# A fused two-block network kernel: the FFN written as two program blocks instead of one, and another order of the group norm around the last scan chunk

## The reference

```
y  = (scan + d_skip * xs) * silu(z)
yg = y * rsqrt(mean(y*y over the group) + eps) * norm_g
x  = x + gate * (yg @ out_w)
```

## Time and profile before

| | |
|---|---|
| median of 3 runs | 1453.96 us (1452.37 to 1456.07) |
| the profiled execution | 1453.96 us, span 1452.2 us |
| PE busy | 94% of the span |
| DVE, ACT, POOL busy | 57%, 41%, 28% |
| mean granted TensorE clock | 0.967 of full speed |
| DMA | 181 MB, mean 125 GB/s |

### The profile page before, as it was taken

How to read it: one execution, slowest core, us unless ns; L and a number is a source line. 1 busy time by engine, 2 the same in 40 slices (tenths; PEclk the granted TensorE clock), 3 DMA queues, 4 the chain that set the end, 5 groups by cost and what they waited for, 6 DMA issues and landing times. The chain is left out here.

```text
span 1452.2 us, 19530 instructions
## 1 busy us (share of the span) xinstructions
PE 1364.5 (94%) x7904; PEld 1080.3 (74%) x7904; DVE 820.9 (57%) x965; ACT 589.0 (41%) x848; POOL 409.3 (28%) x191
## 2 busy tenths in 40 slices
PE   5999789969999999999999998998999999999996
PEld 3777566748888888887778886766777799777775
DVE  3788763476556555333755665776842831565544
ACT  4323445442222222212454346776632422455541
POOL 0000000018987888999200000000000050232220
PEclk9999889979999999999799999999999999999998
DMA  9433035213544545554132333334132342111121
GB/s 390 148 145 117 30 109 182 66 51 120 215 186 166 186 167 222 204 182 174 58 120 87 114 109 105 117 102 151 38 110 88 127 163 88 58 47 42 59 88 58
DMA packets 41350, 181.12 MB, mean 125 GB/s; under 512 B 3392, under 2 KB 20160, under 8 KB 21312
## 3 DMA queue, kind: packets, MB, share of 16 engines
q1 hardware_dynamic: 40128, 171.73, 32.9%
q10 hardware_dynamic: 1152, 8.39, 1.7%
HBM read 173.75 MB, written 6.36 MB: 124 GB/s over the span
## 5 line engine op out<-in xcount | busy, mean ns | idle before, releaser
L193 DVE TENSOR_TENSOR wlo<-raw,whi 128x2048 fp32r<-128x2048 f32 x95 | 253.7, 2670 | 182.2 <-ACT whi L189 179.6
L200 POOL TENSOR_TENSOR ada_raw<-ada_raw,cs 128x2048 f32<-128x2048 f32 x36 | 150.1, 4171 | 504.2 <-DVE h2lo L451 457.5
L271 PE MATMUL ps<-hhi,whi 128*128 128x512 f32 x640 | 252.1, 394 | 2.3 <-PEq L562 0.8
L271 PE MATMUL ps<-hhi,wlo 128*128 128x512 f32 x640 | 249.4, 390 | 0.0
L271 PE MATMUL ps<-hlo,whi 128*128 128x512 f32 x640 | 249.1, 389 | 0.0
L189 ACT ACTIVATE whi<-raw 128x2048 fp32r<-128x2048 f32 x95 | 181.5, 1911 | 143.6 <-PE ps L1303 91.3
L209 POOL TENSOR_TENSOR ada_raw<-ada_raw 128x1024 f32<-128x1024 f32 x72 | 164.4, 2283 | 5.7
L271 PEld LDWEIGHTS ps<-hhi,whi 128*128 128x128 f32 x640 | 120.2, 188 | 28.7 <-issue 2.4
L271 PEld LDWEIGHTS ps<-hhi,wlo 128*128 128x128 f32 x640 | 120.1, 188 | 25.7
L271 PEld LDWEIGHTS ps<-hlo,whi 128*128 128x128 f32 x640 | 120.2, 188 | 24.3
L2030 POOL TENSOR_TENSOR x<-x,rest 128x256 f32<-128x256 f32 (+3 forms) x32 | 49.0, 1531 | 163.8 <-DVE rest L2325 163.8
(11 more groups left out here) (373 smaller groups left out, 2810.1 us busy)
## 6 DMA issues: line engine op xcount, KB each, us to landing
raw<-panels SPq DMA_DIRECT2D x87, 1024.0 KB, 4.9
ada_raw<-ada SPq DMA_DIRECT2D x48, 1024.0 KB, 6.7
first<-ada SPq DMA_DIRECT2D x8, 1024.0 KB, 20.7
bc<-ac_rows SPq DMA_DIRECT2D x32, 256.0 KB, 3.8
raw<-panels ACTq DMA_DIRECT2D x8, 1024.0 KB, 5.1
x_kept<-x SPq DMA_DIRECT2D x2, 2048.0 KB, 9.6
x<-x_kept SPq DMA_DIRECT2D x2, 2048.0 KB, 8.0
x<-x_in SPq DMA_DIRECT2D x1, 2048.0 KB, 9.1
```

Of the source, the lines that this page charges most:

```text
L193: e.tensor_tensor(wlo[:, c % 2, :, :], raw[:, c % 2, :, :], whi[:, c % 2, :, :].bitcast(F32), ALU.subtract).then_inc(lo_split, 1)
L200: e.tensor_tensor(ada_raw[:, c % 2, :, :], ada_raw[:, c % 2, :, :], cs[:, which, :].unsqueeze(2).to_broadcast([P, KT, 256]), ALU.mult).the ...
L271: mm = e.matmul(ps[:, 2 * (qc % 2) + b, :], w[:, c % 2, 2 * k + b, :], src[part][:, k, :], **flags)
```

## The change

**Edit 1, the FFN.** The one block becomes two: one for the input projection, one for the output projection with its norms. Each engine's stream is cut at the same place, between the last input step and the first output panel. The special order of banks in PE's first output panel goes, and so do its three waits and POOL's wait for the pairs ahead of ada block 50. No arithmetic is added or taken away.

**Edit 2, the scan's last chunk and the group norm.** The arithmetic stays; helpers move within the streams of PE, ACT and DVE. The quarters of `z` in the last chunk move from the steps 1, 3, 5, 6 to 1, 2, 4, 6.

```
@@ the FFN
+                c0 = FIRST["ffn_out"]
+                last = c0 + COUNT["ffn_out"] - 1
...
+                with nc.Block() as block:
...
-                            if a == 50:
-                                pool.wait_ge(pair_free[0], 17)
-                                pool.wait_ge(pair_free[1], 17)
...
-                        pe.wait_ge(lo_split, co + 1)
-                        for b in (5, 6, 7, 0, 1, 2, 3, 4):
-                            if b in (0, 2):
-                                pe.wait_ge(pair_free[b // 2], 17)
-                            if b == 4:
-                                pe.wait_ge(mod_read, read_counts[(20, 41)])
-                            for k2 in range(2):
-                                mm = product(co, 0, k2, b, k2)
-                        mm.then_inc(panels_used, 1)
+                        panel(c0, 0, 0)
@@ the scan
-            IN_BATCHES = [(1, 2, 4, 5, 7), (1, 3, 5, 7), (1, 2, 4), (1, 3, 5, 6)]
+            IN_BATCHES = [(1, 2, 4, 5, 7), (1, 3, 5, 7), (1, 2, 4), (1, 2, 4, 6)]
@@ PE, behind the contraction of a step of the last chunk
-                                        if 2 * g + b == 5:
+                                        if 2 * g + b == 4:
                                             squares(0)
                                         if 2 * g + b == 6:
                                             group_spread(0)
-                                        if 2 * g + b == 7:
                                             squares(1)
@@ PE, in m_panel(k), ahead of tile j
-                                if (k, j) == (0, 2):
+                                if (k, j) == (0, 1):
                                     group_spread(1)
...
-                                if (k, j) == (1, 3):
+                                if (k, j) == (1, 2):
                                     squares(3)
-                                if (k, j) == (2, 1):
+                                if (k, j) == (2, 0):
                                     group_spread(3)
@@ ACT, behind decays(n) of the last chunk
-                                if c == TB - 1 and b == 5:
+                                if c == TB - 1 and b == 4:
                                     group_squares(0)
+                                if c == TB - 1 and b == 6:
+                                    group_squares(1)
@@ ACT, behind the scan
-                        group_squares(1)
                         hi_part(act, 0)
                         group_std(1)
                         for p in late:
                             split_hi(act, c0 + p + 2, 0)
+                        for p in range(turned, MT // 2):
+                            silu_z(p)
                         group_squares(2)
                         hi_part(act, 1)
-                        group_std(2)
-                        for p in range(turned, MT // 2):
-                            silu_z(p)
                         for n in range(NN - 5, NN):
                             for p in taken_at(n):
                                 load_panel(act, c0 + p + 4, 0)
-                        hi_part(act, 2)
+                        group_std(2)
                         group_squares(3)
                         split_hi(act, cm + 2, 0)
+                        hi_part(act, 2)
                         group_std(3)
@@ DVE, in the last chunk
-                                    if g < MG - 1 and not (c == TB - 1 and b == 1):
+                                    if g < MG - 1:
                                         masked(n + 2)
-                                    if g < MG - 1 and c < TB - 1:
                                         for p in taken_at(n - 1) if n % NB else ():
                                             split_lo(dve, c0 + p + 2, 0)
...
-                                    if g < MG - 1:
-                                        masked(c * NB + 2 * g + 3)
                                     if g == MG - 2:
                                         group_rs(dve, 0)
+                                    dve.wait_ge(M["yskip"], 4 * gi + 4)
+                                    if g < MG - 1:
+                                        dve.wait_ge(G["z"], 2 * g + 2)
                                     if g == MG - 1:
-                                        for n in range(NN - 3, NN):
-                                            for p in taken_at(n):
-                                                split_lo(dve, c0 + p + 2, 0)
                                         norm_lo(dve, 1)
-                                        group_rs(dve, 2)
-                                    dve.wait_ge(M["yskip"], 4 * gi + 4)
-                                    dve.wait_ge(G["z"], 2 * g + 2)
+                                        dve.wait_ge(G["z"], 2 * g + 2)
                                     gate_part(dve, g)
-                                    if g == 1:
-                                        for n in range(c * NB, NN - 3):
-                                            for p in taken_at(n):
-                                                split_lo(dve, c0 + p + 2, 0)
...
+                        for n in range(NN - 3, NN):
+                            for p in taken_at(n):
+                                split_lo(dve, c0 + p + 2, 0)
+                        group_rs(dve, 2)
+                        split_lo(dve, cm + 2, 0)
                         norm_lo(dve, 2)
-                        split_lo(dve, cm + 2, 0)
                         group_rs(dve, 3)
```

More of the change, by code:

```diff
@@ L1215, in build @@
                 parts = [(0, ADA_C2 - a0), (ADA_C2 - a0, FT - 1)]
[L1216 to L1220, removed]
                 with nc.Block() as block:
@@ L1225, in _ @@
                         load_panel(sp, c0 + 5, (FT - 2) // 2)
[L1227 to L1234, removed]
                     @block.gpsimd
@@ L1255, in _ @@
                         pairs(act, FT, step)
[L1257 to L1260, removed]
                     @block.vector
@@ L1278, in _ @@
                         read_mod(dve, 20, 41)
+                    @block.tensor
+                    def _(pe):
+                        pairs(pe, FT - 1, lambda i, r: (in_panel(pe, c0 + 1 + r, q0 + 1 + r, i, (hhi, hlo), False),
+                                                        ada_columns(pe, a0 + r, i)))
+                c0 = FIRST["ffn_out"]
+                last = c0 + COUNT["ffn_out"] - 1
+                post2 = post_norm("ffn_post", "g2", y_place[:, 0:KT, :], y_place[:, 8:11, :], last, late=(41, 54, sums, [3, 3, 1, 1, 2, 3]))
+                pre2 = pre_norm(v("norm2", 0, KT), "msc", "msh", hhi, hlo, y_place[:, 11:13, :],
+                                ps[:, ORDER[1], :])
+                with nc.Block() as block:
+                    @block.sync
+                    def _(sp):
+                        k = 4
+                        for a in range(43, 54):
+                            while k < 14 and 11.25 * (k - 4) + 7 < 9 * (a - 43):
+                                load_panel(sp, c0 + k, 0)
+                                k += 1
+                            load_ada(sp, a, 0)
+                        for k in range(k, 15):
+                            load_panel(sp, c0 + k, 0)
+                    @block.gpsimd
+                    def _(pool):
+                        for a in range(41, 54):
+                            ada_reduce(pool, a, 0, sums(a))
+                        post2["pool"](pool)
+                    @block.scalar
+                    def _(act):
+                        act.activation(warm[:, 4:5], ones[:, 0:1], ACT.Sqrt)
+                        stream(act, "ffn_out", hi=True, keep_last=1)
+                        post2["act"](act)
+                        pre2["act"](act)
+                    @block.vector
+                    def _(dve):
                         dve.wait_ge(mod_read, read_counts[(20, 41)])
@@ L1307, in product @@
                             return mm
-                        pe.wait_ge(lo_split, co + 1)
-                        for b in (5, 6, 7, 0, 1, 2, 3, 4):
-                            if b in (0, 2):
-                                pe.wait_ge(pair_free[b // 2], 17)
-                            if b == 4:
-                                pe.wait_ge(mod_read, read_counts[(20, 41)])
-                            for k2 in range(2):
-                                mm = product(co, 0, k2, b, k2)
-                        mm.then_inc(panels_used, 1)
+                        panel(c0, 0, 0)
                         with pe.Fori(0, 4) as i:
                             for u in range(2):
-                                panel(co + 1 + u, i, 2 + 2 * u)
+                                panel(c0 + 1 + u, i, 2 + 2 * u)
                         panel(last - 1, 0, FT - 4)
```

5 lines of the change are left out of this document (removed).

## The result

The changed kernel took 1469.71 us (median of 4 runs, 1468.46 to 1476.26); beside it the kernel before took 1453.16 us (4 runs, 1450.76 to 1456.07). The ratio over the runs is 1.0122 with an interval of 1.0086 to 1.0158 (that of the two medians is 1.0114): slower by 16.5 us by the medians. The profiled execution took 1469.33 us, 15.4 more than that of before. The forecast was 1470.0.

What follows compares the result with a forecast made beforehand. PE, 94% busy, was taken as the only engine without room. Edit 1 at 7.7 us plus edit 2 at 8.6 made 16.3, added to 1453.96 for 1470.3, rounded 1470; range 1460 to 1478, forecast's own 1464.5 to 1474.

Steps and rivals of the forecast that it cites:

- The meeting: At the new FFN cut all engines meet, so PE goes on 5.6 us later, after DVE's last step and SP's load.
- The low clock behind it: After the wait at the FFN cut PE runs at 1.2 GHz for a while, costing 2.1 us, bounds 1.7 and 2.4.
- POOL's cover: POOL's late start on block 41 costs nothing; it comes 5 to 6 us nearer to PE, within 6.92 at post norm 2.
- The ring: Last scan chunk: squares waiting for DVE's gates hold up ACT's decay tiles, so PE's spread of group 0 starts 3.4 us late.
- From the spread to panel cm: Between the spread of group 0 and the first output panel the same work follows, 4.76 us, so no added time.
- The wait for group 1's reciprocal: In panel cm the spread of group 1 comes one tile earlier, so PE newly waits 0.8 us.
- The wait for panel cm+1: Its low part now stands behind group 1's norm and group 3's gate on DVE, so PE waits 4.0 us.
- The low clock behind that: After the wait for panel cm+1 PE's clock is low again, costing 2.1 us.
- Old waits gone: PE's waits between 1022.21 and 1063.55 us go, giving back 1.7 us.

Runs made afterwards that it cites:

- The cut with less work left: Edit 1 alone, but DVE's last split and SP's load that waits for it stand behind the cut; 1456.49 us, ratio 1.0012 to the kernel before.
- PE was kept busy: Edit 1 alone, plus 22 extra PE matmuls, never read, behind its last input step; 1461.95 us, ratio 1.0045 to the kernel before.
- POOL at work: Edit 1 alone, but POOL does ada block 41 ahead of the cut; 1461.80 us, ratio 1.005 to the kernel before.
- edit 1 alone: The kernel before with only the FFN cut into two blocks, the scan as before; 1461.51 us, ratio 1.0048.
- edit 2 with the split put back: Edit 2 without edit 1, low part of panel cm+1 again ahead of DVE's norm of group 1; 1457.11 us, ratio 1.0018 to the kernel before.
- The kernel with both losses taken out: Edit 2 without edit 1, squares of groups 0 and 1 and low part of panel cm+1 put back; 1450.76 us, ratio 0.9968 to the kernel before.
- the spreads where they had been: As with both losses taken out, plus spreads of groups 1 and 3 and squares of group 3 a tile later; 1447.62 us, ratio 0.9955.

## Why the prediction was right

*The meeting, 5.6.* Measured 5.55, with all its parts: the step of 4.27 us, SP's load behind it, 0.45 for the meeting. The cut with less work left shows that this is its cause.

*The low clock behind it, 2.1.* Measured 2.0 in two kernels (148.46 and 148.41 us against 146.43), and gone where PE was kept busy or waited less. With POOL at work beside DVE it was 1.6, and kernels without a cut had 146.4 to 147.0 us here, so the term is good to half a microsecond. In the two kernels the pre norm's panel was 1.06 us shorter than before (12.93 against 13.99 us from its first matmul to the next block's). That isn't the change's doing: this length was 12.9 to 14.4 in the kernels run here, with a cut or without, by how long the low clock lasted there (12 matmuls of before started at it, and 6 or 7 of the changed kernel).

*POOL's cover.* It held. POOL waits 6.76 us for its first add at post norm 2, against 6.92 in the earlier trace rows:

```profile
701.12 0.74 POOL L209 TENSOR_TENSOR fg<-ada_raw 128x256 f32<-128x256 f32 x1
708.62 1.27 POOL L433 TENSOR_TENSOR x<-x,y_place 128x512 f32<-128x512 f32 x1 [6.76 <-DVE y_place L419]
```

The forecast had it 5 to 6 us nearer to PE; it came only 0.2 nearer. The groups by line of POOL from 562 to 705 us show why, of before and then of the changed kernel (busy us, mean ns, idle before):

```profile
L200 POOL TENSOR_TENSOR ada_raw<-ada_raw,cs 128x2048 f32<-128x2048 f32 x13 | 54.8, 4214 | 0.8 <-DMA ada_raw<-ada 0.8
```

```profile
L200 POOL TENSOR_TENSOR ada_raw<-ada_raw,cs 128x2048 f32<-128x2048 f32 x13 | 46.9, 3604 | 15.9 <-POOLq L1216 15.9
```

The same 13 products took 7.9 us less: none was held up beside DVE any more, where four of before took 5.4 to 5.7 us instead of 3.6. The short adds behind them (L209) took 3.8 us more in return. In all POOL started block 41 13.5 us later (575.50 against 562.01) and needed 126.4 us instead of 131.4 from there to its last add, so it ended 8.4 later, while PE came 8.3 later. The forecast left POOL's own pace as it was.

*The ring, 3.4.* Measured 3.5: from the first contraction of the chunk to the spread of group 0 it took 28.86 us against 25.33, and 25.34 with edit 1 alone. The ring's links came out one by one, less the 7.10 us by which the whole chunk began later: squares 0 were put at 1004.2 and began at 1004.18, squares 1 at 1013.4 and at 1013.30, the spread at 1020.9 and at 1020.98.

*From the spread to panel cm, 0.* This was mis-sized: 5.83 instead of 4.76 us, since the low clock lasted to 1033.9. It is one of the stretches whose length varies from execution to execution: kernels with the scan as before had 4.71, 5.28 and twice 5.83, and edit 2 with the split put back, which has the same ring and the same work there, 4.73.

*The wait for group 1's reciprocal, 0.8.* It didn't appear: the spread starts at 1036.79, right behind a matmul at 1036.56. The reciprocal ended at 1036.50, within 0.1 of where the forecast had it, but PE came 1.2 us later than the sum had it, nearly all by the term above.

*The wait for panel cm+1, 4.0.* Measured 4.12, and gone when the split alone was put back. The path behind it came out too: the split's end was put at 1043.9 and came, less 7.10, at 1044.24.

*The low clock behind that, 2.1.* Measured 1.4: seven matmuls started 0.43 apart instead of 0.23, from 1051.39 on. The mean of two stretches was too long for this one.

*Old waits gone, 1.7.* They are gone (0.23, 0.75 and 0.71 us). A further 1.0 us between panel cm and the first token sum went that the forecast didn't have. Most of it is in the squares of group 3. PE's timeline, of before and then of the changed kernel:

```profile
1044.88 1.89 PE L1506 MATMUL ps<-ada_raw,consts 128*32 128x128 f32 x32 [0.23 <-ACT ada_raw L1696]
```

```profile
1059.41 1.08 PE L1507 MATMUL ps<-ada_raw,consts 128*32 128x128 f32 x32
```

The granted clock was 1.00 in the row of before: PE took the four squares there as fast as ACT made them, one in 0.61 us. In the changed kernel ACT makes them ahead of the high parts of group 2 instead of behind them and is done 3.9 us before PE comes. The kernel with both losses taken out has this order too and no wait for panel cm+1, and PE's squares take 1.0 us there as well, so it is a gain of the order. The forecast's row of 0.23 showed only the start of this old stall.

The stage's sum is 3.5 + 1.1 + 4.1 + 1.4 - 1.7 - 1.0 = 7.4, where 8.6 was forecast; edit 1 came to 5.55 + 2.0 - 1.06 = 6.5 by the start of the next block, where it was 7.7. That is 13.9 of the 15.3 us between the two spans. Of the rest 0.7 lies ahead of the cut and 0.8 behind the first token sum, stretches where the program is the same, and between the two edits the changed kernel was 0.1 faster. So the two edits account for 13.9 us in this trace where 16.3 was forecast. The mechanisms were right; that the total came within 1 us of the measured one is in part luck, since terms of about a microsecond were off in both directions and stretches without an edit added 1.4.

What the prediction didn't see is that edit 2 is two losses and a gain. It set -1.7 for what edit 2 gives back behind the spread. Ahead of it, it named ACT's wait of 6.09 us that goes, but only inside the net 3.4 of the ring; that without the ring the spread comes 3.2 us earlier than before was not in the forecast. With the losses taken out, the same edit makes the kernel 0.32% faster, and 0.45% with the spreads where they had been.

## What to carry to other kernels

A cut into two blocks cost here what the latest engine still had to do when PE arrived, plus 0.3 to 0.5 us, plus a cold start of PE where that wait was 5.41 us and none where it was 2.64; so move an engine's last work behind the cut before cutting. In an order written by hand, don't put an operation that waits for engine B in front of the work that B's next result needs: two engines then go round in a ring at the sum of their links. When a mixed edit comes out slower, put its moves back one at a time: here the sum of what they cost was more than the loss, and the rest was a gain worth keeping.

## What the runs showed of the hardware

With edit 1's last split moved behind the cut, POOL and DVE start an operation at the same moment. Timeline of POOL and of DVE there:

```profile
572.62 3.61 POOL L200 TENSOR_TENSOR ada_raw<-ada_raw,cs 128x2048 f32<-128x2048 f32 x1 [10.23 <-POOLq L1216]
```

```profile
572.64 5.74 DVE L193 TENSOR_TENSOR wlo<-raw,whi 128x2048 fp32r<-128x2048 f32 x1 [0.32 <-PEq L1216]
```

POOL's ends at 576.23; DVE's, 2.28 long by itself, ends at 578.38, 2.15 behind it. DVE had got next to nothing done until POOL was through: turns, not shares. The Trainium skill (SBUF — State Buffer, section "SBUF: two separate sides") says this of DVE operations with two SBUF inputs against GpSimd ones, and these rows agree. The cast in the kernel with POOL at work has one SBUF input and was held up in the same way, from 0.43 to 1.04 us. All three end behind POOL's operation by some 0.15 us less than they take alone (2.15, 0.28 and 0.54 for 2.28, 0.43 and 0.69).

The clock was granted at 1.00 behind a wait of 2.64 us in dense work and at 0.50 behind waits of 4.12, 4.31 and 5.41 us; one of 5.5 us filled with matmuls whose results nobody reads left it at 1.00. The length of the wait alone doesn't decide: in the scan the clock was at 0.50 behind a wait of 2.47 us in the changed kernel, and behind one of 2.39 us in the kernel before, though it had been 1.00 ahead of both. What makes the difference to the 2.64 us at the cut is not shown.
